# The key and value products of a decoder trunk, ordered by token tile or by weight chunk

## The reference

```python
y = _moe(u, ...)
x = _layer_norm(DEEPNORM_ALPHA * x + (1 + g_m) * y, W['ln_g'][l, 1], W['ln_b'][l, 1])
...
def _shared_kv(x, silu_c, kv_w_mod, kv_b_mod, kv_w, fox_b_f):
    m = (silu_c @ kv_w_mod + kv_b_mod)[:, None, :]
    sh, sc = jnp.split(m, 2, axis=-1)
    p = (x * (1 + sc) + sh) @ kv_w          # 1024 -> 1024 keys, 1024 values, 8 forget gates
    k = p[..., :FOX_DIM]; v = p[..., FOX_DIM:2 * FOX_DIM]
    logf = log_sigmoid(p[..., 2 * FOX_DIM:] + fox_b_f)
```

## Time and profile before

| | |
|---|---|
| median of 3 runs | 2074.85 us (2073.39 to 2082.39) |
| the profiled execution | 2078.39 us |
| its span in the trace | 2076.8 us |
| PE busy | 1684.5 us (81%) |
| DVE busy | 685.8 us (33%) |
| ACT busy | 310.6 us (15%) |
| DMA, mean | 325 GB/s |

### The profile page before, as it was taken

How to read it: one execution, slowest core, us unless ns; L and a number is a source line. 1 busy time by engine, 2 the same in 40 slices (tenths; PEclk the granted TensorE clock), 3 DMA queues, 4 the chain that set the end, 5 groups by cost and what they waited for, 6 DMA issues and landing times. The chain is left out here.

```text
span 2076.8 us, 34005 instructions
## 1 busy us (share of the span) xinstructions
PE 1684.5 (81%) x13065; PEld 1022.8 (49%) x13066; DVE 685.8 (33%) x1821; ACT 310.6 (15%) x665; POOL 355.0 (17%) x453
## 2 busy tenths in 40 slices
PE   6997988487779987774699988887587899987766
PEld 4455655254445554442455666654344455544433
DVE  1211236511423331221711255547312333331126
ACT  0221201110011111100001244331010011110100
POOL 3000100122212222221001011100122122221210
PEclk9999999699999999997799999998799999999996
DMA  9479874699999999994922599995599999999966
GB/s 348 162 273 341 325 291 150 278 419 423 425 384 375 417 422 408 403 387 158 323 107 70 189 297 322 323 344 201 202 423 423 413 417 406 421 418 410 411 249 224
DMA packets 132060, 674.14 MB, mean 325 GB/s; under 512 B 28111, under 2 KB 40527, under 8 KB 91620
## 3 DMA queue, kind: packets, MB, share of 16 engines
q1 hardware_dynamic: 84880, 570.20, 69.5%
q10 hardware_dynamic: 21604, 55.96, 8.0%
q0 software_dynamic: 25456, 46.27, 6.2%
HBM read 651.03 MB, written 46.94 MB: 336 GB/s over the span
## 5 line engine op out<-in xcount | busy, mean ns | idle before, releaser
L2323 PE MATMUL bank<-ring,work 128*64 128x256 f32 x4096 | 481.6, 388 | 107.5 <-DMA ring<-in_exp_w 106.0
L2323 PEld LDWEIGHTS bank<-ring,work 128*64 128x64 f32 x4096 | 327.2, 139 | 298.4 <-issue 117.4
L2335 PE MATMUL bank<-ring,work 128*64 128x512 f32 x1032 | 250.6, 603 | 63.7 <-DVE work L1760 60.3
L811 POOL DMA_INDIRECT work<-u_d,work x128 | 130.6, 1020 | 781.2 <-DVE work L1728 427.2
L2051 PE MATMUL bank<-ring,uT 128*128 128x512 f32 (+1 forms) x896 | 256.1, 501 | 6.4 <-DVE u L1481 4.2
L1728 DVE COPY work<-work 128x1 int32<-128x1 int32 (+1 forms) x128 | 19.3, 153 | 657.3 <-ACT work L1186 656.5
L2051 PEld LDWEIGHTS bank<-ring,uT 128*128 128x128 f32 (+1 forms) x896 | 118.4, 168 | 134.7 <-issue 114.1
L818 POOL DMA_INDIRECT pair_d<-work x128 | 132.4, 1034 | 123.9 <-issue 73.7
L2335 PEld LDWEIGHTS bank<-ring,work 128*64 128x64 f32 x1032 | 73.7, 136 | 150.9 <-issue 145.9
L1180 ACT COPY work<-bank 128x512 f32<-128x512 f32 x128 | 75.1, 587 | 366.7 <-PE bank L2335 366.6
L1186 ACT ACTIVATE work<-bank 128x128 f32<-128x128 f32 x128 | 35.5, 278 | 532.2 <-PE bank L2323 532.2
(11 more groups left out here) (363 smaller groups left out, 1717.8 us busy)
## 6 DMA issues: line engine op xcount, KB each, us to landing
ring<-in_exp_w SPq DMA_DIRECT2D x128, 2048.0 KB, 21.3
ring<-in_exp_w SPq DMA_DIRECT2D x128, 1024.0 KB, 20.8
ring<-in_ada_w SPq DMA_DIRECT2D x24, 2048.0 KB, 11.7
ring<-in_cache_k SPq DMA_DIRECT2D x128, 256.0 KB, 6.9
ring<-in_cache_v SPq DMA_DIRECT2D x128, 256.0 KB, 6.8
ring<-in_gla_w_in SPq DMA_DIRECT2D x6, 2048.0 KB, 17.6
ring<-in_kv_w_mod SPq DMA_DIRECT2D x4, 2048.0 KB, 11.4
work<-pair_d ACTq DMA_DIRECT2D x4, 2048.0 KB, 9.5
```

The lines of the kernel that those rows point to most:

```text
L811: pool.indirect_dma_start(out=xg[:, s, :], out_offset=None, in_=u_d, in_offset=bass.IndirectOffsetOnAxis(ap=xi[:, s:s + 1], axis=0), bound ...
L2323: ins = mm(psum[s][64 * c:64 * c + 64, 0:2 * P].rearrange("p (a n) -> p a n", a=2), xT[:, s, j * P + 64 * half:j * P + 64 * half + 64], gu ...
L2335: ins = mm(psum[3 + s][64 * c:64 * c + 64, :], hT[:, s, 64 * f:64 * f + 64], w[:, f, c * 512:(c + 1) * 512], start=(f == 0), stop=(f == 1) ...
```

## The change

The products are made tile by tile where keys are concerned: a list `KEY_JOBS` holds (0,0), (1,0), (0,1), (1,1), (0,2), (1,2), and the value products follow chunk by chunk as before. TensorE turns tiles 0 and 1, makes their forget gates and their four key products, and then turns tile 2, makes its gates and goes on; the six key turns start only there, one ahead of each of the next six products. ScalarE issues `w_small` directly behind the pair loads, takes the square roots of tiles 0 and 1, copies the turned tiles 0 and 1, and takes the square root of tile 2 after the copy of the first key product; the modulation loads come after the copies of turned tile 2. VectorE makes the second modulation between the second and the third key copy. `load_pairs` no longer ends with the square roots; the last MoE's are written out behind its call.

```diff
--- before.py
+++ after.py
@@ -148,7 +148,9 @@
 
 Y_STORED = [[(l + 1) * len(range(s, NE, 3)) for s in range(3)] for l in range(2)]
 
-KV_SLOTS = [((j, t), 3 * j + t if j < 2 else (6 + j - 2 if t == 2 else None)) for j in range(4) for t in range(3)]
+KEY_JOBS = [(j, t) for t in range(3) for j in range(2)]
+KV_SLOTS = [(job, n) for n, job in enumerate(KEY_JOBS)]
+KV_SLOTS += [((j, t), 6 + j - 2 if t == 2 else None) for j in (2, 3) for t in range(3)]
 GROUPS = 2 * DB
 
 
@@ -454,7 +456,7 @@
         plan_jobs += [("w_in", j, t) for t in range(3) for j in range(GLA_FIRST, W_IN_N // 512)]
         plan_jobs += [("gla_wo", j, t) for t in range(3) for j in range(2)]
         plan_jobs += [("comb", 0, t) for t in range(3)]
-        plan_jobs += [("kv", j, t) for j in range(4) for t in range(3)] + [("w_q", h) for h in range(FH)]
+        plan_jobs += [("kv", j, t) for (j, t), _ in KV_SLOTS] + [("w_q", h) for h in range(FH)]
         plan_jobs += [("fox_wo", j, t) for t in range(3) for j in range(2)]
         plan_jobs += [("comb", 1, t) for t in range(3)]
         lin = BankRing(sem, "lin", [0, 1, 5], plan_jobs,
@@ -467,7 +469,7 @@
             if s in ("moe0", "moe1"):
                 turn_jobs += [("places", int(s[-1]))]
             if s == "kv":
-                turn_jobs += [("kT", j, t) for j in range(2) for t in range(3)]
+                turn_jobs += [("kT", j, t) for j, t in KEY_JOBS]
         turn = BankRing(sem, "turn", [3, 4], turn_jobs)
         alone = [n for n in range(ADA_N) if not FIRST_ADA <= n < FIRST_ADA + sum(ADA_AFTER)]
         adas = BankRing(sem, "ada", [2, 6], range(ADA_N), {n: 0 for n in alone})
@@ -1253,7 +1255,6 @@
                     act.dma_start(y_pairs[n][0:r, :, :],
                                   dram(pair_d, (t0 * TOPK + 4 * half) * D, [[TOPK * D, r], [1, 4 * D]]))\
                        .then_inc(sem(f"pairs_loaded{n}"), 16)
-                std(2 * l + 1)
 
             moe_front(0)
             experts(0)
@@ -1261,11 +1262,17 @@
             load_pairs(0)
             act.dma_start(w_small[:, :, 0:FH], W["kv_w_rest"][0].rearrange("p (c n) -> p c n", c=KT))\
                .then_inc(sem("router_loaded"), 16)
-            u_ready(act, "kv", 2)
-            load_modulation(3, 1, "a")
-            turned("kv")
+            std_tile(1, 0)
+            std_tile(1, 1)
+            turned_tile("kv", 0)
+            turned_tile("kv", 1)
 
             for (j, t), slot in KV_SLOTS:
+                if (j, t) == (1, 0):
+                    std_tile(1, 2)
+                if (j, t) == (0, 2):
+                    turned_tile("kv", 2)
+                    load_modulation(3, 1, "a")
                 if (j, t) == (3, 0):
 
                     wait(act, "lf_neg_ready", 1)
@@ -1282,7 +1289,7 @@
                         n_before = (slot - 4) // 4 + 1
                         act.wait_ge(sem(f"kv_out{slot % 4}"), 16 * n_before)
                         if slot - 4 < 6:
-                            turn.wait_full(act, ("kT",) + KV_SLOTS[slot - 4][0])
+                            turn.wait_full(act, ("kT",) + KEY_JOBS[slot - 4])
                     dst = kv_rows[0:r, slot % 4, :]
                 for cols, src in lin_pieces(job, t):
                     ins = act.copy(dst[:, cols], src)
@@ -1372,6 +1379,7 @@
             experts(1)
             overflow(1)
             load_pairs(1)
+            std(3)
             for t in range(2):
                 act.wait_ge(sem("ln_done"), 9 + t + 1)
                 act.dma_start(O["y_prompt"][0, t * P:(t + 1) * P, :], x[:, t, :]).then_inc(sem("y_out"), 16)
@@ -1863,16 +1871,16 @@
             combine(0, 2)
 
 
-            turn.wait_full(dve, ("kv", 2, 1))
-            modulate(3)
-            for j in range(2):
-                for t in range(3):
-                    t0, r = TILES[t]
-                    job = ("kT", j, t)
-                    turn.wait_full(dve, job)
-                    src = psum[turn.bank(job)][:, :].rearrange("p (h n) -> p h n", h=4)[:, :, 0:r]
-                    dst = kTp[:, 4 * j:4 * j + 4, t0:t0 + r] if t < ST else kTs[:, 4 * j:4 * j + 4, :]
-                    dve.tensor_copy(dst, src).then_inc(turn.is_free(job), 1)
+            for j, t in KEY_JOBS:
+                t0, r = TILES[t]
+                if (j, t) == (0, 1):
+                    turn.wait_full(dve, ("kv", 2, 1))
+                    modulate(3)
+                job = ("kT", j, t)
+                turn.wait_full(dve, job)
+                src = psum[turn.bank(job)][:, :].rearrange("p (h n) -> p h n", h=4)[:, :, 0:r]
+                dst = kTp[:, 4 * j:4 * j + 4, t0:t0 + r] if t < ST else kTs[:, 4 * j:4 * j + 4, :]
+                dve.tensor_copy(dst, src).then_inc(turn.is_free(job), 1)
             turn.wait_drained(dve, ("kT", 1, 2))
             wait(dve, "lf_full", 1)
             run.do(dve.memset(lf[:, :, :], 0.0))
@@ -2436,16 +2444,17 @@
             combine(0)
 
 
-            turn_stage("kv")
-            pe.wait_ge(sem("router_loaded"), 48)
-            for t, (t0, r) in enumerate(TILES):
+            def forget_gates(t):
+
+                t0, r = TILES[t]
+                turn.wait_drained(pe, ("kv", t, 1))
                 for c in range(KT):
                     ins = mm(psum[(2, 6, 7)[t]][0:r, 0:FH], uT[:, c, t0:t0 + r], w_small[:, c, 0:FH],
                              start=(c == 0), stop=(c == KT - 1))
-            ins.then_inc(signal("lf_full"), 1)
+                return ins
 
             def turn_new_keys(j, t):
-                slot = (3 * j + t) % 4
+                slot = KEY_JOBS.index((j, t)) % 4
                 r = tile_rows(t)
                 lin.wait_freed(pe, ("kv", j, t))
                 job = ("kT", j, t)
@@ -2455,13 +2464,21 @@
                                        kv_rows[0:r, slot, i * P:(i + 1) * P], ident[0:r, 0:r])
                 ins.then_inc(turn.is_full(job), 1)
 
-            for j in range(4):
-                unit = weights_landed(pe, ("kv", j))
-                for t in range(3):
-                    product(("kv", j, t), t, unit)
-                    n = 3 * j + t - 1
-                    if 0 <= n < 6:
-                        turn_new_keys(n // 3, n % 3)
+            turn_tile("kv", 0)
+            turn_tile("kv", 1)
+            pe.wait_ge(sem("router_loaded"), 48)
+            forget_gates(0)
+            forget_gates(1)
+            new_keys = iter(KEY_JOBS)
+            for (j, t), _ in KV_SLOTS:
+                if (j, t) == (0, 2):
+                    turn_tile("kv", 2)
+                    forget_gates(2).then_inc(signal("lf_full"), 1)
+                if t == 2 or j >= 2:
+                    job = next(new_keys, None)
+                    if job:
+                        turn_new_keys(*job)
+                product(("kv", j, t), t, weights_landed(pe, ("kv", j)))
             turn_stage("fox")
             wait(pe, "lf_ready", 1)
             mm(psum[2][:, 64:64 + FH], upto[:, :], lf[:, 0, :], start=True, stop=True)
```

## The result

Beside 22 executions of the kernel before (median 2079.84 us, 2068.26 to 2084.23) the changed kernel took 2067.95 us in the median of 22 (2053.03 to 2088.38). The ratio is 0.9948 with an interval of 0.9932 to 0.9964: about half a per cent less, 11.9 us by the medians and 10.8 by the ratio, and not the 18 us that were forecast. One of the 22, the 2088.38, ran in a slower state than the others and does not enter the ratio. Two things stand out beside the median. The new times spread twice as wide as the old. And the 2074.85 us that the forecast started from was a median of three; of 22 it is 5.0 us higher.

The account below looks back on a forecast made before the run. TensorE, held through ScalarE's late copy of tile 0, bounds this stretch. First product 1020.96, tile 2 turned 1050.3, plus 49.7 gives 1100.0 against 1117.95: 18.0 us off the 2074.85 median, 2056.9 us; range 2053 to 2074.5.

Parts of the forecast that it names:

- The hold on ScalarE: ScalarE's late copy of turned tile 0 delays tile 1's turn; freed, the gap is 0.32 us, first product at 1020.96.
- The start of the narrow matmuls: Gates of tiles 0 and 1 on TensorE: `w_small` lands by 1012, so they follow tile 1's turn without waiting.
- rival A: DMA queues alternate one for one, `w_small` lands near 1030.3; gain only 1.4 us, 2073.5 us; chance 0.22.
- Rival B: DMA queues take turns of about 16 pieces, `w_small` lands near 1023; gain 8.7 us, 2066.2 us; chance 0.07.
- Half clock: If TensorE's clock is at half, the 32 narrow matmuls cost 5.85 us and not 3.68, 2.2 more.
- Four products: TensorE's key products of tiles 0 and 1: 4 x 6.96 = 27.84 us, plus 1.5 for a possible half clock.
- T: The time at which TensorE turns tile 2, behind the four key products: 1050.3; from there 49.7 us to the attention stage.
- The deviation of tile 2 behind the first key copy: Tile 2's square root on ScalarE waits until about 1028.6; tile ready near 1031, 19 us early, at no cost.
- The modulation loads: Issued behind T + 2.1, 11.2 us to first use; third key copy done at T + 21.4, 5 us of cover.
- rival D: Modulation loads land later than T + 18.6 and stall TensorE from the fifth key turn; possibly 2078 us; chance 0.04.
- Rival C: Something in the attention stage not released by TensorE keeps back half the gain: 2066 us; chance 0.05.

Follow-up runs that it names:

- second trace: The changed kernel once more, unedited: no wait for `w_small`, stretch from the turn of tile 0 to the attention stage 83.2 us, span 2059.7 us.
- the late load: Changed kernel with the load of `w_small` moved back behind ScalarE's first copy of turned tile 0: 2075.77 us, ratio 0.9985 to before.
- fourth trace: The changed kernel a fourth time, unedited: wait of 12.1 us for `w_small`, stretch 99.4 us, span 2080.0 us.
- first trace: The changed kernel's first profiled execution: wait of 4.8 us for `w_small`, stretch 91.6 us, span 2072.2 us.
- early-load kernel: Changed kernel with `w_small` loaded in the middle of the first MoE layer's expert loop instead of behind the pair loads: 2061.26 us, ratio 0.9926 to before.
- Four kernels: Changed kernel with `w_small` loaded early (2061.26 us), packed into 128 pieces (2062.31), both plus gates behind four products (2061.59), or only gates behind them (2066.96).
- the gates behind the products: Changed kernel with the first four products ahead of the narrow matmuls of tiles 0 and 1: 2066.96 us, ratio 0.9941 to before.
- these two: Kernel before with ScalarE's new order only: 2075.45 us, ratio 0.999; changed kernel with ScalarE's old hold, TensorE's new order kept: 2079.27 us, ratio 0.9997.

## Why the prediction was wrong

- **The hold on ScalarE, and what its end brings.** Right: the gap ahead of tile 1's turn is 0.32 in every trace of the changed kernel. First product forecast 6.13 us after the turn of tile 0; without a wait it came after 6.07 (second trace, 1029.52).
- **The start of the narrow matmuls: the step that failed.** "Then the small pieces ... are taken while the last pairs move and before q1's first, and they land by 1012." That held for fifteen engines. One was late with the pairs in all four traces, and in three of them some or all of its small pieces fell into the alternation, which the prediction had as rival A and took to be a matter of all engines or none. A load is complete with its slowest engine; the sum had none. The cost was 0, 4.8, 8.1 and 12.1 us of wait, and 3.2 of clock with any of them: 6.3 and 2.4 on the mean, 8.7 of the 18.9 that the change gives where nothing waits. This mean is what the sum lacks: 18.0 less 8.7 is 9.3, and the four stretches gained 9.9. The late engine stood in the trace of before already: "by about 1007 q10 comes to these pieces" is true of fifteen, but in 1008 to 1009, with the weights on their way since 1006.98, q10 still began a pair piece (1008.17):

```profile
q1 hardware_dynamic: 19, 0.31, 86.5%
q10 hardware_dynamic: 1, 0.02, 7.1%
```

The late start that the prediction read from the earlier trace rows is real and is no protection: the late load had its first packet 4.1 us after its issue began, and went one for one from there.
- **Rival A, 0.22.** Its mechanism is the right one for the late engine, and `w_small` against the weights was rightly named as the place of least certainty. Its stretch, 1116.6 - 1014.8 = 101.8, is nearly the fourth trace's (99.4). As a case for every run it was too long by 9.6 on the mean.
- **Rival B, 0.07.** Its gain of 8.7 is close to what came, for another reason. The Trainium skill, "DMA: Bandwidth & Descriptors", section "Queues, rings and completion order", has an engine drain a whole packet of, typically, some 9 to 17 descriptors before it switches. No such turns show here while both queues have work on the late engine. Equal totals alone would allow them, but the pieces come evenly: four in 1024 to 1026 and four in 1026 to 1028 of the first trace, where a turn of 9 large pieces would, by an estimate of 9 times 0.61, leave 5.5 us without any. In those 2 us an engine moves 3.3 large ones. The 44, 64 and 38 small pieces that went in a row before q1's came between fit neither 9 to 17 nor one, and stay open.

```profile
q1 hardware_dynamic: 55, 0.88, 103.7%
q10 hardware_dynamic: 4, 0.00, 0.1%
```

- **Half clock.** The sum took 5.85 us for 32 narrow matmuls at half clock, two thirds of before's 48 in 8.78. Three traces of the changed kernel say 7.00, too little by 1.15: the 16 of tile 2 have 64 rows and are cheaper (1.07 us at full clock, where 32 of 128 rows take 3.77), so two thirds of 48 is not the price of 32.
- **Four products, and T.** Forecast 27.84 + 1.5 = 29.3; measured 29.27 to 29.98 in the changed kernel (27.63 and 28.27 where the gates stand behind). T came 35.3 us after the turn of tile 0 in the second trace, forecast 35.5. From T to the attention stage the forecast was 49.7 with 1.0 for the clock; measured 48.0 in all four traces (1115.68 - 1067.72), and 51.2 in the early-load kernel, where the clock fell. The whole stretch, forecast 85.2: 83.2 without a wait.
- **The deviation of tile 2 behind the first key copy** (1048.25): nobody was late, right. It came 24.1 us after the turn of tile 0, forecast 13.8; 8.1 of the 10.4 are the products' late start (14.25 for 6.13).
- **The modulation loads, rival D.** From first issue to first use 12.5 us, forecast 11.2 (it answers to the earlier trace rows); the third key copy was done at T + 21.6 (forecast 21.4), and TensorE asked for its bank at T + 26. No wait:

```profile
1081.40 1.23 DVE L1429 SCALAR_TENSOR_TENSOR u<-mscale,x 128x1024 f32<-128x1024 f32 x1 [5.21 <-DMA mshift<-mod_d]
...
1088.58 1.27 DVE L1883 COPY work<-bank 128x512 f32<-128x512 f32 x2
...
1093.76 0.46 PE L2463 MATMUL bank<-ident,work 64*128 64x64 f32 x4
```

- **Rival C, the gain passed on.** From the attention stage's first turn to the end: 949.9 to 958.9 in three traces of before, mean 954.7; 953.0 to 960.8 in four of the changed kernel, mean 955.9. Passed on whole, within that noise.
- **The numbers.** The forecast of 2057.0 lies 10.95 under the measured 2067.95. Of this 5.0 is the base (2074.85 of three runs, 2079.84 of 22) and 6.1 the gain (18.0 less 11.9), with rounding. With the base of 22 runs the forecast would have been 2061.9. Four kernels have no wait for these weights in their traces: three measured 2061.3, 2062.3 and 2061.6, the fourth, with the gates behind the products, 2067.0. The range, 2053 to 2074.5, held the time; but 0.66 for faster by over 0.5% was too sure, since the ratio's interval (0.9932 to 0.9964) lies on both sides of that bound. It is also added up wrongly: 0.62 and a fifth of 0.12 are 0.64, and what is left for within is 0.32, not 0.30. That the measured time lies between the forecast and rivals A and B says little for either, since one program takes now the short way and now the long one.

## What to carry to other kernels

In these traces a load made of many tiny pieces, once it stood beside a stream of large ones, went one piece for one on each DMA engine, and was as late as its slowest engine. Where a new order asks for such a load sooner, lay it down without gaps or issue it a stage earlier; count its pieces per engine and multiply by the time of one large piece, as far as the large stream lasts (here 64 pieces meet 32 large ones of 0.61 us, 20 us at the worst; behind them the rest goes at once). When the times of a change spread wider than those of its base, take more than one trace before explaining the median. And two edits that each remove one of two conditions may each measure as nothing, as these two did.

## What the runs showed of the hardware that was not expected

- The sixteen DMA engines did not finish the pair loads together. In the fourth trace one began its last 16 KB piece at 1012.69, the others by 1010.83. Such a late engine is in all four traces of the changed kernel, and with it a wait of anything from 0 to 12 us: its lateness (1.9, 1.6, 1.8, 1.5 us in the fourth, first, second and third) does not decide how much.
- TensorE's granted clock fell from 1.00 to about 0.5 in some executions, as in the early-load kernel at 1062 (6.17 us for a product of 3.67), and not in others with the same instructions and the same idle times ahead of them (0.80 us at most). With the gates behind the products it fell without any idle time of TensorE shown ahead. Why is open.
- One place where executions part by several us is the very start, where SyncE issues the first 2 MB weight loads: an issue took 7.70 us in the first trace of before and 11.89 in that of the changed kernel, in code that is the same. The first turn in front of the first MoE stage was then 7.8 us apart (355.73 and 363.56), the turn of tile 0 9.3. How much of it is this issue, no run shows.

```profile
7.03 7.70 SPq L614 DMA_DIRECT2D ring<-in_ada_w  x1
```

```profile
6.88 11.89 SPq L616 DMA_DIRECT2D ring<-in_ada_w  x1
```

What stays open: why one engine lags with the pairs, whether it is always the same, what decides how many small pieces it moves in a row, and whether the gates behind the products, with a stretch as short as any, are slower than the early load (2067.0 and 2061.3, with intervals that overlap) or only measured so.
